# Two transformer layers on one core: units moved between the steps of a chain, dt's chain moved into the attention, the last expert's rows added by a one-hot product

## The chip, the cores and the metric

The kernel runs on 1 core of a Trainium2 chip. The metric is the device time of one execution in microseconds (us). A core has TensorE (matmul, PE in the profile; its loading of weights is PEld), VectorE (DVE), ScalarE (ACT), GpSimd (POOL) and SyncE (SP), which here only issues DMAs. All engines run their own instruction streams and wait for each other by semaphores. TensorE's clock is granted at one of two levels here, 1.2 or 2.4 GHz.

## The reference, cut to what matters

```python
# layer 1: adaLN, mLSTM + sparse attention, then a mixture of 32 experts, 4 of them for each of 256 tokens
logits = xf @ w_router + b_router;  vals, idx = top_k(logits, 4);  gate = softmax(vals)
y2[token] = sum over its 4 experts e of gate * (swiglu(h2 @ w_up[e] + b_up[e]) @ w_down[e] + b_down[e])
x = x + gt2 * rmsnorm(y2, g_post_ffn)
# layer 2: one input projection, then two branches side by side
h = rms_norm(x, norm_g) * (1 + scale) + shift;   proj = h @ w_in
q, k, v, z_att, q_idx, k_idx, w_idx, z_ssm, xbc, dt_raw, gate_logits = split(proj)
o_att = sparse_attention(rope(rms_norm(q)), rope(rms_norm(k)), v, index scores, top 64 keys) * silu(z_att)
y_att = o_att @ w_branch_att
xbc = silu(causal_depthwise_conv(xbc));  xs, bm, cm = split(xbc)
dt = softplus(dt_raw + dt_bias);  a = -exp(a_log)
y = (ssd(xs, dt, a, bm, cm) + d_skip * xs) * silu(z_ssm);  y = rms_norm over 4 groups(y)
y_ssm = y @ w_branch_ssm
merged = sigmoid(g_att) * y_att + sigmoid(g_ssm) * y_ssm
x = x + gate * (merged @ w_out)
```

256 tokens, D = 1024, all fp32; w_in of layer 2 is 1024 x 10084, ssd works in 2 chunks of 128 tokens, 32 heads, 4 groups.

## The kernel before, in words

The program is a row of blocks, one after another; in a block each engine has its own hand-written order, and a block ends when all engines have ended (the next block's first instructions follow some 0.5 us later).

**Experts** (L1340 to L1638). 32 experts, each with a fixed room of 96 rows. For each expert TensorE makes `up` (L1428), `turn` (L1439) and `down` (L1451) from weights that SP streams in; VectorE clips (`swiglu`, L1559 to L1566) and copies the result from PSUM to `ye` (`copy_y`, L1570); ScalarE stores `ye` to `y_dram` (`store`, L1517). GpSimd gathers each token's four rows from `y_dram` (L1398) in the order of `PLACES` (3, 2, 1, 0: place 3 is the token's lowest expert, place 0 its highest); VectorE multiplies them by the gates and adds (`add`, L1576, L1579), adds the bias product (`add_bias`, L1587), ScalarE squares (L1544), and so to the norm (L1486) and the next layer's norm.

**Units of layer 2.** All its weights go as units of 1024 x 256 (1 MB) through a ring of `RAWS` = 3 buffers (`load_unit`, L289, on SP). A unit in `SPLIT` is cut by ScalarE into a rounded part (`make_high`, L1655) and by VectorE into the rest (`make_low`, L1662), and TensorE makes three products of the rounded type from it; the buffer is free after `make_low`. A unit in `PLAIN` is multiplied as fp32, and its buffer is free only when TensorE has used it. Both are L1686 (by tokens) and L1698 (by columns), 48 instructions a split unit, 32 a plain one. `STAGES` = 3 pairs of high and low.

**Attention block** (L1822 on). Between the steps of the attention TensorE gives units (`give`), ScalarE takes them (`take`: silu to `azT` for four z units, L1861; four scaled copies, L1872, and later silu, L1849, for twelve xbc units), and GpSimd convolves (L1835). The order on TensorE before: give 2, turn index q and k, give 3, turn q and k (L1970), logits and scores 0, give 3, logits and scores 1, give 4, turn probabilities, give 2, turn, turn, give 2, attention product (L1995). VectorE multiplies `azT` by it at the end.

**State space block** (L2128 on). xbc is turned to token rows in nine sets (L2196, copies L2156), dt is made from 25 small VectorE operations (L2262 to L2279) to `adt`, `y = xs * dt` for all (L2286). Then eight pairs (chunk c, group g): `prepare` (L2213, L2216) makes the segment sums, VectorE the segment (L2306), ScalarE its exp (L2165), VectorE M (L2315), TensorE y (L2252); between them 16 fills, which are units for z and the two gates. After the pairs fills 16 to 19 (`w_branch_att`), gated into `mer` (L2353).

**Last block** (L2350 on). y is turned (L2384) and split into yh and yl (L2417, L2441), eight units of `w_branch_ssm` (L2394), merge (L2452 to L2455), four units of `w_out`, the addition to xT (L2461), turn (L2406) and output.

## Time and profile before

| what | us |
|---|---|
| median of 3 runs (lowest, highest) | 1860.7 (1860.04, 1865.69) |
| the profiled execution, whole | 1861.18 |
| its span | 1859.4 |
| TensorE busy | 1740.1 (94%) |
| VectorE, ScalarE, GpSimd busy | 555.9, 415.5, 106.4 |
| experts | about 289 to 1360 |
| layer 2 | about 1379 to 1859 |

Mean granted clock of TensorE 0.972 of 2.4 GHz. A row of the timeline gives start and length in us, engine, line, operation, written tile and read tiles, shapes and count, and in brackets the idle time before it with what ended it. A busy time of matmuls is modelled at its end, so the distance between starts says more than the length. A row of windows gives, for a stretch, its length and then each engine's busy time in it.

### The profile page before, as it was taken

The page shows a single profiled execution, that of the slowest core. Times are in us where ns is not written, and L with a number is a line of the kernel's source. Part 1 is how long each engine was busy: PE and PEld are TensorE (multiplying, and loading weights), DVE is VectorE, ACT ScalarE, POOL GpSimd, SP SyncE. Part 2 cuts the span into 40 slices and gives each one's busy share as a digit, 9 for nine tenths or more (in the row PEclk, how much of TensorE's full clock was granted, in tenths as well). Part 3 has the DMA queues.
Part 4 walks back from the last instruction along what each step waited for, and adds up shares of the span by engine and source line. Part 5 has one row for each costly group of instructions (what it writes and reads, how often), then busy time and mean ns, then how long its engine had stood idle before and what let it go on. Part 6 is the DMA issues. An engine that isn't in the chain of part 4 may idle for free. (4 is left out here: it accounts for less than half of the span.)

```text
span 1859.4 us, 39736 instructions
## 1 busy us (share of the span) xinstructions
PE 1740.1 (94%) x17331; PEld 1017.3 (55%) x17331; DVE 555.9 (30%) x770; ACT 415.5 (22%) x692; POOL 106.4 (6%) x121
## 2 busy tenths in 40 slices
PE   6999998999999999999999999999859798799888
PEld 4875652343434434343443434344449787698888
DVE  2273172121111112111111211111346551676754
ACT  2344152000000000000000000000034266355442
POOL 0111020000000000000000000000000044110000
PEclk9999989999999999999999999999979899899999
DMA  9987395999999999999999999999616243333452
GB/s 344 345 286 244 133 338 210 388 396 407 401 397 399 399 398 395 400 398 393 392 403 404 394 399 397 399 398 408 226 51 196 63 135 93 113 116 112 136 148 80
DMA packets 187878, 545.45 MB, mean 293 GB/s; under 512 B 16216, under 2 KB 90216, under 8 KB 154952
## 3 DMA queue, kind: packets, MB, share of 16 engines
q1 hardware_dynamic: 172432, 519.49, 74.0%
q10 hardware_dynamic: 10968, 15.40, 2.3%
q0 software_dynamic: 4416, 9.69, 1.6%
q8 instruction: 44, 0.72, 0.2%
q14 instruction: 18, 0.15, 0.0%
HBM read 526.06 MB, written 17.84 MB: 293 GB/s over the span
## 5 line engine op out<-in xcount | busy, mean ns | idle before, releaser
L1428 PE MATMUL ps<-ring_low,xg 128*32 128x512 f32 x3072 | 344.6, 597 | 0.0
L1428 PE MATMUL ps<-first_ring,xg 128*32 128x512 f32 x3072 | 335.4, 592 | 0.0
L1559 DVE TENSOR_SCALAR gl<-ps 128x768 f32<-128x768 f32 x32 | 30.6, 957 | 684.1 <-PE ps L1428 684.1
L1428 PEld LDWEIGHTS ps<-first_ring,xg 128*32 128x32 f32 x3072 | 99.5, 110 | 230.1 <-issue 230.1
L1428 PEld LDWEIGHTS ps<-ring_low,xg 128*32 128x32 f32 x3072 | 96.4, 110 | 206.6 <-issue 200.8
L1451 PE MATMUL ps<-first_ring,aT 128*32 128x256 f32 x3072 | 173.3, 382 | 2.3 <-ACT aT L1510 2.3
L1451 PE MATMUL ps<-raw_more,aT 128*32 128x256 f32 x3072 | 171.6, 379 | 0.0
L1451 PEld LDWEIGHTS ps<-first_ring,aT 128*32 128x32 f32 x3072 | 100.4, 111 | 82.5 <-issue 20.2
L1504 ACT ACTIVATE sg<-gl 128x768 f32<-128x768 f32 x32 | 27.0, 844 | 510.8 <-DVE gl L1559 510.8
L1451 PEld LDWEIGHTS ps<-raw_more,aT 128*32 128x32 f32 x3072 | 99.9, 110 | 65.9
L1662 DVE TENSOR_TENSOR low<-ring_low,high 128x2048 fp32r<-128x2048 f32 x42 | 98.7, 2350 | 121.5 <-ACT high L1655 121.0
L1509 ACT ACTIVATE aT<-ps 128x576 f32<-128x576 f32 x32 | 20.8, 650 | 445.5 <-PE ps L1439 435.7
L1655 ACT ACTIVATE high<-ring_low 128x2048 fp32r<-128x2048 f32 x42 | 80.4, 1915 | 65.8 <-PE ps L2394 20.5
L1570 DVE COPY ye<-ps 128x768 f32<-128x768 f32 x32 | 30.6, 957 | 212.1 <-PE ps L1451 212.1
L1698 PE MATMUL ps<-hT,ring_low 128*128 128x256 f32 x384 | 86.1, 386 | 0.0
L1698 PEld LDWEIGHTS ps<-hT,ring_low 128*128 128x128 f32 x384 | 74.5, 195 | 10.6 <-ACT xbc L1872 0.3
L1398 POOL DMA_INDIRECT got<-y_dram,dest x8 | 7.6, 952 | 1075.8 <-DMA y_dram<-ye 1074.6
L1698 PE MATMUL ps<-inh,high 128*128 128x256 f32 x320 | 49.0, 293 | 16.1 <-ACT azT L1861 7.8
L321 PE MATMUL ps<-hT,first_ring 128*128 128x256 f32 x256 | 58.7, 389 | 1.8 <-ACT hT L514 1.8
L321 PEld LDWEIGHTS ps<-hT,first_ring 128*128 128x128 f32 x256 | 49.2, 194 | 11.5 <-issue 4.7
L1698 PEld LDWEIGHTS ps<-inh,high 128*128 128x128 f32 x320 | 43.2, 198 | 17.1 <-ACT azT L1861 8.1
L1835 POOL TENSOR_TENSOR xbc<-xbc,taps 128x512 f32<-128x512 f32 x36 | 46.1, 1279 | 102.5 <-ACT xbc L1872 100.5
(487 smaller groups left out, 1879.6 us busy)
## 6 DMA issues: line engine op xcount, KB each, us to landing
first_ring<-in_w_up_dram SPq DMA_DIRECT2D x128, 1024.0 KB, 6.6
ring_low<-in_w_up_dram SPq DMA_DIRECT2D x128, 1024.0 KB, 6.3
raw_more<-in_w_down_dram SPq DMA_DIRECT2D x64, 1024.0 KB, 6.7
first_ring<-in_w_down_dram SPq DMA_DIRECT2D x64, 1024.0 KB, 6.7
ring_low<-in_w_in_dram SPq DMA_DIRECT2D x39, 1024.0 KB, 5.3
first_ring<-in_w_ada_dram SPq DMA_DIRECT2D x7, 2048.0 KB, 20.3
ring_low<-in_w_ada_dram SPq DMA_DIRECT2D x5, 2048.0 KB, 18.2
y_dram<-ye ACTq DMA_DIRECT2D x32, 288.0 KB, 5.7
```

The costliest lines, as they stand in the source:

```text
L321: mm = pe.matmul(ps[:, bank, (j % 2) * SEQ:(j % 2 + 1) * SEQ], slots[n % len(slots)][:, k, j * P:(j + 1) * P], src[:, k, :], start=(k == 0 ...
L1398: pool.indirect_dma_start(got[:, t, BUFFER[j], :], None, y_dram[0:TOTAL, :], bass.IndirectOffsetOnAxis(dest[:, t, j:j + 1], 0))\
L1428: mm = pe.matmul(ps[32 * q:32 * q + 32, u, :], xg[:, k, 32 * block_of:32 * block_of + 32], w[:, :, 256 * f:256 * f + 256], start=False, st ...
L1451: mm = pe.matmul(ps[32 * q:32 * q + 32, 5 + u, 0:256], aT[:, f, 32 * block_of:32 * block_of + 32], w[:, 256 * part:256 * part + 256], star ...
L1504: act.activation(sg[:], gl[:], ACT.Sigmoid, scale=ALPHA).then_inc(s(tag, "sig_ready"), 1)
L1509: act.activation(aT[:, 0:6, :], flat[:, :, 0:ROWS], ACT.Copy).then_inc(s(tag, "aT_ready"), 1)
L1559: dve.tensor_scalar(gl[:], ps[:, 0:3, 0:256], LIMIT, None, ALU.min).then_inc(s(tag, "glu_ready"), 1)
L1570: dve.tensor_copy(ye[:], ps[:, 5:8, 0:256]).then_inc(s(tag, "ye_copied"), 1)
L1655: act.activation(high[:, s_ % STAGES], raw2[u % RAWS], ACT.Copy).then_inc(sm("u_high"), 1)
L1662: dve.tensor_tensor(low[:, s_ % STAGES], raw2[u % RAWS], high[:, s_ % STAGES].bitcast(F32), ALU.subtract)\
L1698: mm = pe.matmul(ps[:, bank, j * SEQ:(j + 1) * SEQ], a[:, k, j * P:(j + 1) * P], x[:, k, :], start=(i == 0), stop=(i == len(todo) - 1))
L1835: ins = pool.tensor_tensor(c, c, taps[:, i % 2, tap], ALU.add)
```

## The change

- The order of units in layer 2: two z units, then the twelve xbc units, then the other two z units. Unit 7 (100 columns wide) and the first two units of `w_branch_att` (40, 41) are plain now. 39 units are split, where 42 were.
- The attention: give 2, turn index, give 2, turn q, give 1, logits and scores 0, give 3, logits and scores 1, give 4, turn, give 2, turn, give 1, turn, give 1, product. ScalarE takes both first z units before it squares the second half of q. dt's chain stands in this block, on VectorE before the scores and after the probabilities. Only three columns of the taps are cleared. Gating azT has moved to the next block.
- The state space block: cumulative products first, the nine sets in another order over three banks, copied by ScalarE (six) and VectorE (three), fill 0 before the first `prepare`, y multiplied pair by pair. Fills 16 and 17 read azT unsplit; 18 and 19 go to the last block, between the turns of y.
- Output: the first output unit does six row blocks of both column halves, then two.
- Experts: the last expert's rows are not stored. A one-hot of its rows times gate (`picks`, `picks3`) is made and turned ahead of the first expert, and the rows are added to the bias product in PSUM; place 0 is gathered behind place 1 with a gate that is zero for those tokens. VectorE adds place 1 before it copies the last expert's result. ScalarE fetches the Sqrt table during the last expert.

```diff
-UNITS2 += halves("w_in_2", 0, P_ZA) + halves("w_in_2", 0, P_ZA + 512)
+UNITS2 += halves("w_in_2", 0, P_ZA)
 U_XBC = len(UNITS2)
 UNITS2 += sum((halves("w_in_2", 0, P_XBC + 512 * n) for n in range(6)), [])
+UNITS2 += halves("w_in_2", 0, P_ZA + 512)
-PLAIN = {0, 1} | set(range(U_XBC, U_ZS))
+PLAIN = {0, 1, U_ZA - 1} | set(range(U_XBC, U_ZS - 2)) | {U_ATT, U_ATT + 1}
...
                 for j in PLACES:
-                    pool.wait_ge(s("", "ye_stored"), 32 * (NE - j))
+                    pool.wait_ge(s("", "ye_stored"), 32 * (NE - max(j, 1)))
...
+                def last_rows():
+                    for t in range(TT):
+                        at = slice(t * P, (t + 1) * P)
+                        pe.matmul(ps[:, 2 * t, :], picks[:, at], ye[0:ROWS, 0:2, :].rearrange("p u n -> p (u n)"),
+                                  start=False, stop=True, skip_group_check=True)
+                        pe.matmul(ps[:, 2 * t + 1, 0:256], picks[:, at], ye[0:ROWS, 2, :], start=False, stop=True,
+                                  skip_group_check=True)
+                        for u in range(3):
+                            mm = pe.matmul(ps[:, 2 * t + 1, 256:512], picks3[:, u, at], ye[ROWS:P, u, :], start=False,
+                                           stop=(u == 2), skip_group_check=True)
+                        mm.then_inc(s("", "bias_summed"), 1)
+                pe.wait_ge(sm("hot31_ready"), TT)
+                for t in range(TT):
+                    at = slice(256 + t * P, 256 + (t + 1) * P)
+                    pe.matmul(ps[0:ROWS, 5, at], li[:, t, 0:ROWS], idn, start=True, stop=True)
+                    for u in range(3):
+                        mm = pe.matmul(ps[ROWS:P, 5 + u, at], li[:, t, 32 * u:32 * u + 32], idn, start=True, stop=True)
+                mm.then_inc(sm("hot31_turned"), 1)
                 up("", 0)
...
                 turn("", NE - 1)
+                pe.wait_ge(sm("bdn_in"), 16)
+                down_bias(range(3), False)
                 down("", NE - 1)
-                pe.wait_ge(sm("bdn_in"), 16)
-                down_bias("")
+                down_bias(range(3, 4), False).then_inc(s("", "bias_started"), 1)
+                pe.wait_ge(s("", "bias_started"), 1)
+                pe.wait_ge(s("", "ye_copied"), NE + 1)
+                last_rows()
...
                 turned("", NE - 1)
-                store("", NE - 1, 0, NE - 1)
+                act.activation(sg[:, 0, 0:1], cst[:, C_ONES:C_ONES + 1], ACT.Sqrt).then_inc(s("", "sig_ready"), 1)
...
                 add("", 3)
                 add("", 2)
+                add("", 1)
                 dve.wait_ge(s("", "ye_stored"), (NE - 1) * 32)
                 copy_y("", NE - 1)
-                add("", 1)
+                add("", 0)
                 add_bias("")
-                add("", 0)
...
# attention block, ScalarE
-                    make_high(act, U_ZA + 2)
                     act.wait_ge(sm("var_ready"), 1)
                     S.done(act, act.activation(var[:], var[:], ACT.Sqrt), sm("dev_ready"))
-                    for t in range(TT):
-                        S.done(act, act.activation(sq2[:], qkv[:, t, 0:NH * HD], ACT.Square), sm("head_sq"))
-                        if t == 0:
-                            make_high(act, U_ZA + 3)
-                        act.wait_ge(sm("head_sums"), t + 1)
-                    S.done(act, act.activation(ssum[:], ssum[:], ACT.Sqrt), sm("head_rms"))
+                    S.done(act, act.activation(sq2[:], qkv[:, 0, 0:NH * HD], ACT.Square), sm("head_sq"))
                     take(2)
                     act.wait_ge(sm("i_turned"), 1)
...
-                    take(3)
+                    act.wait_ge(sm("head_sums"), 1)
+                    S.done(act, act.activation(sq2[:], qkv[:, 1, 0:NH * HD], ACT.Square), sm("head_sq"))
+                    act.wait_ge(sm("head_sums"), 2)
+                    S.done(act, act.activation(ssum[:], ssum[:], ACT.Sqrt), sm("head_rms"))
+                    take(2)
...
# state space block, TensorE and VectorE
+                    pe.wait_ge(sm("az_gated"), 1)
+                    fill(0)
+                    pe.wait_ge(sm("xs_ready"), 6)
+                    pe.wait_ge(sm("xs_copied"), 3)
                     prepare(0)
                     for i, (c, g) in enumerate(PAIRS):
-                        fill(2 * i)
+                        if i:
+                            fill(2 * i)
...
-                    for t in range(TT):
-                        yv = y[:, t, :].rearrange("p (h q) -> p h q", h=SH)
-                        ins = dve.tensor_tensor(yv, xs[:, t, :].rearrange("p (h q) -> p h q", h=SH),
-                                                dts[:, t, :].unsqueeze(2).to_broadcast([P, SH, SP]), ALU.mult)
                     for i, (c, g) in enumerate(PAIRS):
+                        V.link(dve, dve.tensor_tensor(heads(y[:, c, gw]), heads(xs[:, c, gw]),
+                                                      dts[:, c, gh].unsqueeze(2).to_broadcast([P, GH, SP]), ALU.mult))
...
# last block, TensorE
+                    turn(range(4))
+                    unit_by_columns(pe, U_ATT + 2, 4, None, (inh, inl))
+                    turn(range(4, 8))
+                    unit_by_columns(pe, U_ATT + 3, 5, None, (inh, inl))
```

## Rows read from the trace of the kernel before

**Rows 1.** Windows: us of PE, PEld, DVE, ACT, POOL; PEclk, DMA share, GB/s.
```profile
320.00:1300.00 980.00, 980.00 (x12094) 401.76 (x12086) 140.86 (x150) 77.29 (x150) 2.00 (x2) 1.00 1.00 398
...
1430.00:1584.10 154.10, 132.16 (x707) 118.74 (x707) 69.37 (x142) 81.42 (x178) 48.71 (x37) 0.93 0.31 96
1584.10:1620.40 36.30, 28.78 (x194) 26.20 (x195) 22.27 (x36) 14.95 (x20) 5.87 (x3) 0.83 0.45 138
1620.40:1723.30 102.90, 99.89 (x795) 94.09 (x794) 73.56 (x75) 51.21 (x42) 9.51 (x5) 1.00 0.37 114
1723.30:1780.50 57.20, 43.47 (x338) 41.59 (x337) 43.04 (x48) 28.47 (x31) 0.00 (x0) 0.94 0.46 133
```

**Rows 2.** Waits of PE, 1300 to 1860: who for whom; total, times, longest.
```profile
PE ps L1486 <- DVE gl L1627: 14.7, 1, 14.7
...
PE ps L1698 <- ACT azT L1861: 7.8, 1, 7.8
PE ps L2213 <- DVE y L2286: 6.7, 1, 6.7
PE ps L1953 <- ACT qT L1905: 4.6, 1, 4.6
PE ps L2196 <- PEq L1822: 4.4, 1, 4.4
...
PE ps L1938 <- ACT kT L1894: 3.5, 1, 3.5
PE ps L1698 <- issue: 3.4, 1, 3.4
```

**Rows 3.** Windows: unit 7, a split unit of the pair loop, a piece of half clock.
```profile
1424.54:1430.00 5.46, 5.46 (x50) 5.33 (x48) 2.29 (x1) 1.91 (x1) 0.00 (x0) 1.00 0.59 187
1612.00:1617.84 5.84, 5.84 (x52) 5.84 (x51) 4.52 (x2) 0.25 (x1) 2.07 (x1) 1.00 0.58 180
1433.00:1435.00 2.00, 2.00 (x11) 2.00 (x10) 1.86 (x5) 1.72 (x2) 1.10 (x1) 0.50 1.02 329
```

**Rows 4.** Timeline of the attention block: four plain units back to back.
```profile
1508.74 27.79 PE L1698 MATMUL ps<-hT,ring_low 128*128 128x256 f32 x128
```

**Rows 5.** Timeline at the start of the experts.
```profile
289.22 1.47 PE L1422 MATMUL ps<-bup,one 96*32 96x512 bf16 x12 [5.03 <-ACT xg L1500]
```

**Rows 6.** Timeline at the end of the experts, ScalarE.
```profile
1355.85 1.06 ACT L1544 ACTIVATE xsel<-hT 128x1024 f32<-128x1024 f32 x1 [0.82 <-DVE hT L1579]
...
1357.35 1.28 ACT L1547 ACT_TABLE_LOAD   x1 [0.36 <-DVE ssq L1623]
1358.65 0.20 ACT L1547 ACTIVATE ssq<-ssq 128x2 f32<-128x2 f32 x1
```

**Rows 7.** DMA issues, 1334.5 to 1336: median us from issue to landing.
```profile
got<-y_dram,dest POOLq DMA_INDIRECT x2, 7.7
```

**Rows 8.** Timeline of the attention block, VectorE: first and last of 18 on q.
```profile
1451.51 0.28 DVE L2034 RECIPROCAL ssum<-ssum 128x20 f32<-128x20 f32 x1 [0.41 <-ACT ssum L1885]
...
1462.26 0.32 DVE L1816 TENSOR_TENSOR qkv<-rt 128x160 f32<-128x160 f32 x1
```

**Rows 9.** Timeline, VectorE: a 128x1024 product alone and beside GpSimd.
```profile
1453.35 1.23 DVE L2038 TENSOR_TENSOR qkv<-qkv,bc 128x1024 f32<-128x1024 f32 x1
...
1524.11 2.23 DVE L2077 TENSOR_TENSOR sq<-sq,es 128x1024 f32<-128x1024 f32 x1
```

**Rows 10.** Timeline at the start of the state space block, VectorE.
```profile
1593.55 6.03 DVE L2286 TENSOR_TENSOR y<-xs,dts 128x2048 f32<-128x2048 f32 x2
```

**Rows 11.** Timeline of the pair loop: `prepare` of the fourth pair.
```profile
1644.07 0.49 PE L2213 MATMUL ps<-xbc 128*128 128x128 f32 x2 [0.46 <-DVE xbc L2306]
```

**Rows 12.** Timeline behind the pairs, VectorE: y scaled.
```profile
1749.77 4.62 DVE L2344 TENSOR_TENSOR y<-y,gs 128x2048 f32<-128x2048 f32 x2
```

**Rows 13.** Timeline at the end: the last two xT.
```profile
1853.14 1.00 DVE L2461 SCALAR_TENSOR_TENSOR xT<-ps,mod,xT 128x256 f32<-128x256 f32 x2 [4.75 <-PE ps L1698]
```

**Rows 14.** DMA issues, 1329 to 1331: median us from issue to landing.
```profile
ring_low<-in_w_in_dram SPq DMA_DIRECT2D x2, 1024.0 KB, 15.3
```

More of the change, by code:

```diff
@@ L1311, in _ @@
                     V.link(dve, dve.tensor_single_scalar(flag[:], fl, float(ROWS), ALU.is_gt))
+                    V.link(dve, dve.memset(first_row, 0))
                     for r in range(PER):
@@ L1829, in _ @@
                 def _(pool):
-                    G.done(pool, pool.memset(taps[:], 0.0), sm("taps_zero"))
-                    for i in range(HALVES - ZHALVES):
-                        pool.wait_ge(sm("half_taken"), ZHALVES + i + 1)
+                    G.done(pool, pool.memset(taps[:].rearrange("p a b c t -> p (a b c) t")[:, :, 0:3], 0.0), sm("taps_zero"))
+                    for i in range(XBC1 - XBC0):
+                        pool.wait_ge(sm("half_taken"), XBC0 + i + 1)
                         c = xbc[:, 2 * i:2 * i + 2, :]
@@ L1915, in _ @@
                     turned(2, P0[:, :, P:SEQ])
+                    take(1)
                     turned(3, P1)
-                    take(2)
-                    for i in range(HALVES - ZHALVES - 2, HALVES - ZHALVES):
-                        silu(i)
+                    take(1)
                 @block.tensor
@@ L2254, in _ @@
                         mm.then_inc(sm("y_made"), 1)
-                    for f in range(16, 20):
+                    for f in range(16, 18):
                         fill(f)
@@ L2321, in _ @@
                         make_low(dve, U_ZS + 2 * i + 3)
-                        if i == len(PAIRS) - 1:
-                            dve.wait_ge(sm("in_high"), 2)
-                            V.done(dve, dve.tensor_tensor(inl[:], azT[:], inh[:].bitcast(F32), ALU.subtract), sm("in_low"))
                         dve.wait_ge(sm("y_made"), i + 1)
@@ L2338, in _ @@
                     V.done(dve, dve.tensor_scalar(gs[:], gs[:], 1.0 / GW, EPS, ALU.mult, ALU.add), sm("gs_ready"))
-                    make_low(dve, U_ATT + 2)
+                    dve.wait_ge(sm("in_high"), 2)
+                    V.done(dve, dve.tensor_tensor(inl[:], azT[:], inh[:].bitcast(F32), ALU.subtract), sm("in_low"))
                     dve.wait_ge(sm("gs_rms"), 1)
```

274 lines of the change are left out of this document (155 added, 119 removed).

## The prediction, made before the changed kernel ran

> **What bounds the kernel now.** I read the windows by stage first, since one share of busy time over 1859 us says nothing about a stage of 50. In the expert loop TensorE works all 980 of 980 us at the full clock [rows 1]. The change touches that loop nowhere, and none of the waits listed for TensorE lies in it. The second layer is different: TensorE works 132.2 of 154.1 us around the attention, 28.8 of 36.3 at the start of the state space part, 99.9 of 102.9 in its pair loop and 43.5 of 57.2 from the last pair to the branch product [rows 1]. So TensorE sets the end everywhere, and what can be won is what it waits. The list of its waits gives the four places that the change is about: 14.7 us after the experts, 7.8 behind ScalarE's azT, 6.7 behind VectorE's y, 4.6 behind a copied probability tile [rows 2]. A wait costs more than its length. After the block change at 1430 the clock stood at half, 1.2 GHz, in 1433 to 1435 [rows 3]; half speed for some 3.4 us costs 1.7 us. I take 1.7 for every wait above 1.5 us that goes or comes.
>
> Unit prices. A unit that is not split takes 27.8/4 = 7.0 us of TensorE, a split one 5.8, with 1.9 of ScalarE and 2.3 of VectorE besides [rows 3, 4]. I walk through the change in order of time, always in the times of before; a sum at the end collects the differences.
>
> **Start of the experts.** TensorE now first turns the one-hot of the last expert: 8 fp32 products of 128 columns. Nothing in the trace is like it at half speed; from the prices of a unit (32 instructions of 256 columns in 7.0 us) one instruction of 128 columns takes 0.11, and 0.22 at half speed, so 16 take 3.5 us. It can begin at about 288.2, while the first product of the experts began at 289.22, released by ScalarE's xg [rows 5]. It is late by 2.5 us, less about 0.7 because the clock rises earlier: **+1.8** (bounds: 0 if it fits before xg, +2.5). The four small VectorE operations before it are hidden: they are under 1 us together, and behind the last of them ScalarE still had a bias copy and an xsel copy to make; if they were not, they would cost that 1 us.
>
> **End of the experts.** Before, the last expert's rows go to memory and are gathered back; the squares of the second half start at 1355.85, then a table load of 1.28, root, diagonal, and TensorE, 14.7 us after its last bias product, at 1359.8 [rows 2, 6]. After, the rows are added from SBUF by products, and the gather of place 0 no longer waits for a store. If the rows were all that counted: last copy at 1343.1, products 2 x 2.6 us (for each half of the tokens one of 512 columns and four of 256, at the 0.43 that 256 columns cost in a plain unit), 1348.3, addition 1.3, square 1.25, then 1.2 of root and diagonal without the table load, which is fetched earlier: TensorE at 1352.4, 7.4 us gained. But VectorE now adds place 1 **before** it copies the last expert's result, and the gather of place 1 landed late, 7.7 us after issue in the median of its two, of which the second was issued at 1334.8: at about 1342.7 [rows 7]; unit loads and the last weights fill the queues then. So: addition until 1344.0, copy until 1345.0, TensorE has idled since 1341.2 and works the products at half clock, 7.0 us, until 1352.1, addition 1353.3, square 1354.6, TensorE at 1356.2: **-3.6** (bounds -7.4 and -1.5, the latter if two more gathers behind it make the landing 2 us later).
>
> **First projections.** Unit 7 is no longer split: 5.46 us before [rows 3]; 32 instructions of 100 columns at 0.11 (48 took 5.46) make 3.7. The block ended with VectorE's copy right behind it, and SP's next load, now behind this unit instead of behind its low part, is issued in 0.4 us: **-1.7** (0 to -2.7, the latter if columns alone counted).
>
> **Attention.** The work of TensorE is the same: four split units, twelve plain, the small products. What moves are the waits.
> - The wait of 7.8 [rows 2] was for azT, and azT was behind the squares of q, which waited for VectorE's index chain and two splits. Now ScalarE takes azT straight after the first square, and two plain units, 14.1 us, lie under the norm and rotation of q. That chain ran from 1451.5 to 1462.6 [rows 8]. Its root now waits for a square that is behind azT and iqT, plus a table load: 1451.4, the same time. TensorE comes to the turning of q at 1459.6 and waits until 1462.6: 3.0 us.
> - GpSimd now convolves the first xbc unit, 4 us, at 1456 to 1460, beside this chain, where before it began at 1476. Beside such an operation VectorE's 128x1024 product took 2.23 instead of 1.23 [rows 9]. Two such delays: +2.0 (0 to 4.0). The Trainium skill says the same of the mechanism (GPSIMD Engine Reference, Specifications): GpSimd shares its SBUF interfaces with VectorE and contends with instructions that have two SBUF inputs; by it the chain would not be slowed where an operand is in PSUM, which none here is.
> - The wait of 3.5 before the index logits goes under the unit given between; the one of 4.6 goes under unit 22, since ScalarE turned the probabilities in 1.0 us and has the length of a unit for it.
> - Against that stands a rule of the Trainium skill (ScalarE: Activation LUTs, What ACT_TABLE_LOAD costs): a switch of tables costs a drain of about 1.38 us beside the load of 1.28. The change adds one switch for the second root and one for exp(A). The trace does not agree: the load of 1.28 began at 1357.35 and the root behind it at 1358.65, 0.02 after its end [rows 6]. By the page the root would come 1.4 later and the wait be 4.4 instead of 3.0.
>
> Sum: waits of 15.9 (7.8 + 3.5 + 4.6) become 5.0, three half-clock stretches become one: -10.9 - 3.4 = -14.3. The end: the gating of azT (2.3 us) and the last silu stood between the last product and the next block, 4.4 us of waiting [rows 2]; now the block closes 0.6 behind TensorE: -3.8. Further, the index chain loses 2 us of contention with a memset of 3072 columns, hidden. Unhidden remains a piece of half clock at the next start, which I don't count. With 0.9 kept back for ScalarE's heavier end: **-17.2** (bounds: -21 without contention or wait, -9 if ScalarE paces the last four units).
>
> **Start of the state space part.** It took 36.3 us from 1584.1 to 1620.4 [rows 1]. dt's 25 small operations ran in the shade of the transposes, but y for both halves, 6.0 us, stood in front of the first product [rows 10], and that then ran at half clock. After: cumulative products 0.9, nine sets of transposes with copies on two engines 5 (paced by VectorE, which gates azT first, 2.3), fill 0 5.8, preparation 2.4, state product 1.0, wait for the segment 0.7, preparation 2.3, fill 1 5.8, offset and y products 2.6: 26.5. **-9.9** (bounds -12 and -6; the last if all transposes run at half clock).
>
> **Pair loop.** y's product is now made pair by pair: 0.75 by the old row (6.03/8), 0.69 by xd's; 0.72. Is it hidden? The next preparation waited 0.46 us for VectorE's segment although a whole fill lay between [rows 11]: VectorE's chain from y to segment is the longer path by that much in each of pairs 1 to 6. So nothing hides it: 6 x 0.72 = **+4.3** (0 to +10).
>
> **Last pair to branch product.** Unit 40 is no longer split, so ScalarE and VectorE have no split in front of the last M, and TensorE no longer waits for that one. Units 40 and 41 read azT itself, so TensorE does not wait for inh and inl (3.4) [rows 2] and goes on, 2 x 7.0. VectorE then has inl 2.3, the scaling of y 4.6 [rows 12], two low parts 4.6 and two gatings: it ends at 1754.9, 4.1 us after TensorE, and sets the block's end. Behind it units 42 and 43 lie between the transposes, which took 11.4 us with their copies before unit 44; after it 17.5 with both units in them (half clock 1.9, twice 2.0, twice 5.8). Branch product at 1772.9 instead of 1780.5, and at full clock from its start (1.7): **-9.3** (bounds -12 and -5).
>
> **Tail.** The first output unit does six rows of both columns before the last two: -0.8. The last four xT instead of two wait for the last unit, two more operations of 0.5 [rows 13]: +1.0. **+0.2**.
>
> Sum: 1.8 - 3.6 - 1.7 - 17.2 - 9.9 + 4.3 - 9.3 + 0.2 = -35.4. The profiled execution took 1861.2 (span 1859.4, 1.8 around it), half a microsecond over the median 1860.7. So 1825.3, which I put at **1825.5**.
>
> **Rivals.**
> - *The forecast*, with its own range 1815 to 1835: 0.66.
> - *The new order of the attention moves the wait instead of filling it*: contention takes all of GpSimd's time, and ScalarE, with the same copies and more table loads, gives bank after bank late. For it speaks that ScalarE is the engine named in three of the four waits [rows 2]; against it that it works 81 of 154 us there [rows 1]. The stage gives 9 instead of 17.2: 1834. 0.14.
> - *VectorE becomes the bound of the pair loop*: it works 73.6 of 102.9 us [rows 1], so by sum it has room, but by chain it has none. If the added product also delays the split of the next unit, each of six pairs loses 2.5 us more: +15, 1840. 0.12.
> - *The one-hot product does not shorten the end of the experts* (gathers land later still, half clock): no gain there, 1829. 0.06.
> - *Slower: the ring of three raw buffers.* A plain unit holds its buffer until its product is done, so its successor's load has only two plain units, 14.1 us. The list of waits names no DMA [rows 2], so loads land in time now; where the queues were full two of them took 15.3 us [rows 14]. At a landing of t each of twelve units loses t - 14.1. The change would be slower by over 0.3% only from t = 14.1 + 41/12 = 17.5 us on; then +41 - 35, that is 1866. Before, the same twelve plain units showed no such wait. 0.02.
>
> The range takes 1810 (all lower bounds that don't exclude one another) to 1841: **1811 to 1841**. 0.3% is 5.6 us, which three runs within 5.7 us can about tell from no change. Faster by more: 0.95; within: 0.03; slower: 0.02.
>
> **What would show it.** TensorE begins with 16 small products before the first expert; its wait after the experts falls to about 4 + 4 around the last products; the first wait in the attention is about 5 us before the turning of q (128x128 of qkv), none behind azT; the first xd follows a 128x512 product of 0.7 us; the wait before the segment products in the loop is 1.1 to 1.2 instead of 0.4; VectorE's two last gatings end some 4 us behind unit 41. Wrong would be: a wait of the unit products for a DMA, pairs longer than 18 us on average, or gathers that land after 1345.

## The result, and the profile after

| what | us |
|---|---|
| before, median of 4 runs | 1863.1 (1860.0 to 1865.7) |
| after, median of 4 runs | 1836.9 (1834.5 to 1838.5) |
| ratio, 95% interval | 0.9854 (0.9842 to 0.9867) |
| the profiled execution of after, its span | 1836.7, 1834.9 |

The change takes 26.3 us off; forecast were 35.4 off (1825.5), with a range of 1811 to 1841. Between the two profiled executions lie 24.5 us (1861.2 to 1836.7).

Both totals hide losses. Windows of the trace of after for the attention block, the start of the state space block and the pair loop, as in [rows 1]; us of PE, PEld, DVE, ACT, POOL, then PEclk, DMA share, GB/s:

```profile
1435.18:1571.69 136.51, 126.90 (x707) 114.35 (x707) 82.93 (x166) 83.97 (x181) 48.98 (x36) 0.96 0.40 123
1571.69:1598.39 26.70, 24.59 (x194) 22.53 (x195) 15.88 (x15) 12.69 (x15) 5.70 (x3) 1.00 0.49 152
1598.39:1705.66 107.27, 100.02 (x794) 94.08 (x794) 77.90 (x82) 51.21 (x42) 9.53 (x5) 1.00 0.38 118
```

The first window begins with the block's first product. That of [rows 1] begins 1.6 us earlier, with a wait at the change of blocks that after has too (1.62); its block's first product in before:

```profile
1431.63 1.23 PE L1698 MATMUL ps<-inh,high 128*128 128x256 f32 x8 [1.63 <-PEq L1715]
```

So the attention block takes 136.5 instead of 152.5 us and the start of the state space block 26.7 instead of 36.3. The pair loop takes 107.3 instead of 102.9: TensorE works as long as before, and idles more. TensorE's waits in after, as in [rows 2] (who for whom; total, times, longest):

```profile
PE ps L1735 <- PEq L220: 9.7, 1, 9.7
PE ps L2027 <- DVE qkv L1870: 9.3, 1, 9.3
PE ps L2433 <- PEq L2202: 7.0, 1, 7.0
PE ps L1524 <- DVE gl L1676: 5.4, 1, 5.4
PE ps L2277 <- DVE xbc L2357: 5.3, 7, 1.1
PE ps L1494 <- DVE li L1635: 5.3, 1, 5.3
PE ps L1482 <- DVE ye L1612: 4.3, 1, 4.3
...
PE ps L2305 <- DVE xd L2348: 2.8, 3, 0.9
```

The four waits of before are gone. New are one of 9.3 in front of the turning of q, one of 7.0 at the start of the last block, 4.3 in front of the one-hot product, and ten small ones in the pair loop. The first row, 9.7 at the start of layer 2, is the same in both kernels.

**End of the experts.** Timeline of after:

```profile
1343.38 1.28 DVE L1622 SCALAR_TENSOR_TENSOR hT<-got,gate,hT 128x1024 f32<-128x1024 f32 x1 [9.38 <-DMA got<-y_dram,dest]
1346.38 1.28 DVE L1622 SCALAR_TENSOR_TENSOR hT<-got,gate,hT 128x1024 f32<-128x1024 f32 x1 [1.71 <-DMA got<-y_dram,dest]
1347.58 0.95 DVE L1612 COPY ye<-ps 128x768 f32<-128x768 f32 x1
...
1348.68 2.05 PE L1482 MATMUL ps<-ye,picks 96*128 96x512 f32 x2 [4.29 <-DVE ye L1612]
...
1357.22 2.92 PE L1487 MATMUL ps<-ye,low_high 32*128 32x256 f32 x6
...
1363.07 1.28 ACT L1589 ACT_TABLE_LOAD   x1 [0.36 <-DVE ssq L1672]
```

The copy of the last expert's result stands behind two additions that wait for gathers. TensorE has been idle for 4.3 us then and makes the products from 1348.7 to 1360.1, 11.4 us, at half clock (granted 0.50 over this stretch; two instructions of 512 columns in 2.05 us). And the Sqrt table, fetched at 1332.3, is loaded again in front of the root. Between them stands one more table load, behind the branch and in front of the squares:

```profile
1334.16 1.28 ACT L1586 ACT_TABLE_LOAD   x1 [0.33 <-issue]
```

**The q chain.** Timeline of after, VectorE and GpSimd:

```profile
1457.40 0.33 DVE L1866 TENSOR_TENSOR rt<-qkv,sin 128x160 f32<-128x160 f32 x1
1457.76 1.43 DVE L1867 TENSOR_TENSOR rt<-qkv,cos 128x160 f32<-128x160 f32 x1
1459.23 1.31 DVE L1868 TENSOR_TENSOR rt<-qkv,sin 128x160 f32<-128x160 f32 x1
1460.58 1.31 DVE L1869 TENSOR_TENSOR qkv<-rt 128x160 f32<-128x160 f32 x1
1461.92 0.33 DVE L1870 TENSOR_TENSOR qkv<-rt 128x160 f32<-128x160 f32 x1
```
```profile
1457.75 3.95 POOL L1889 TENSOR_TENSOR xbc<-xbc,taps 128x512 f32<-128x512 f32 x3 [22.63 <-ACT xbc L1929]
1464.66 4.23 POOL L1889 TENSOR_TENSOR xbc<-xbc,taps 128x512 f32<-128x512 f32 x3 [2.96 <-ACT xbc L1929]
```

Three additions of GpSimd, three VectorE operations of 1.3 to 1.4 us instead of 0.33; the second three meet three more. The chain takes 17.0 us from the reciprocal to the end, where it took 11.1 [rows 8].

**The last block's start.** Timeline of after:

```profile
1733.05 6.47 SPq L291 DMA_DIRECT2D ring_low<-in_w_branch_ssm_dram  x3
1735.48 1.40 DVE L2401 TENSOR_TENSOR ring_low<-ring_low,ps 128x512 f32<-128x512 f32 x2
...
1739.96 3.65 PE L2433 MATMUL ps<-cst,y 128*128 128x128 f32 x16 [6.95 <-PEq L2202]
```

TensorE is done at 1733.0, VectorE at 1736.9, and the block closes only behind SP, whose three issues last until 1739.5.

**Start of the experts.** Timeline of after:

```profile
286.12 1.91 ACT L1243 ACTIVATE bup<-b 32x2048 bf16<-32x2048 f32 x1 [1.26 <-DVE b L1303]
...
289.88 0.74 PE L1494 MATMUL ps<-cst,li 128*96 128x128 f32 x2 [5.25 <-DVE li L1635]
...
293.08 0.62 PE L1436 MATMUL ps<-bup,one 96*32 96x512 bf16 x3
```

ScalarE now waits 1.26 us for VectorE's last split of b_up, which the small operations on the last expert's rows precede; and the expert's own products start 3.9 us behind [rows 5], 1.3 of which lie ahead of every change (next paragraph).

**A caution for all stage times.** With the same code, layer 1 ended over 4 us apart between profiled executions (the first step of the norm before the router at 235.0 in before, 236.1 in after, 239.4 in the kernel of the first experiment, which has before's code up to there), with more half clock in 150 to 240 in the later ones (mean granted clock 0.96, 0.94 and 0.92). Stage times below are therefore counted from the scaled hT of that norm (VectorE, 128x256 x8, at 248.90 in before and 250.17 in after), so 1.3 us of the later starts in after belong to no change.

### The profile page after: what moved, and what is told of

Read it like the earlier page. It is cut to its first block and busy times, and to the rows that moved or that the text cites. A ratio compares the mean times of both kernels' runs of the same rounds, so it can differ in the third digit from the quotient of the medians.

```text
span 1834.9 us, 39709 instructions
## 1 busy us (share of the span) xinstructions
PE 1740.6 (95%) x17319; PEld 1014.9 (55%) x17319; DVE 565.7 (31%) x784; ACT 413.1 (23%) x691; POOL 106.6 (6%) x121
## 5 line engine op out<-in xcount | busy, mean ns | idle before, releaser
L1711 DVE TENSOR_TENSOR low<-ring_low,high 128x2048 fp32r<-128x2048 f32 x39 | 91.4, 2346 | 75.2 <-ACT high L1704 74.8
L1704 ACT ACTIVATE high<-ring_low 128x2048 fp32r<-128x2048 f32 x39 | 74.7, 1915 | 45.3 <-PE ps L2451 17.3
L348 POOL DMA_DIRECT2D mrows<-mrow x56 | 28.0, 508 | 187.1 <-ACT mrow L341 187.1
L1453 PEld LDWEIGHTS ps<-cst,gl 128*128 128x128 f32 x192 | 20.4, 140 | 26.4 <-issue 26.4
```

Source lines behind the costliest of these rows:

```text
L348: eng.dma_start(mrows[at:at + 4, :], mrow[32 * q:32 * q + 1, i % 2, :].rearrange("a (j p) -> a j p", p=P))\
L1704: act.activation(high[:, s_ % STAGES], raw2[u % RAWS], ACT.Copy).then_inc(sm("u_high"), 1)
L1711: dve.tensor_tensor(low[:, s_ % STAGES], raw2[u % RAWS], high[:, s_ % STAGES].bitcast(F32), ALU.subtract)\
```

## Experiments

In this table: the ratio to the runs of before made together with it, with its interval, and lengths in us, read from each profiled execution: from the scaled hT to the copy of expert 30's result (start), from there to TensorE's products for the norm (end), from there to the first turn of xbc in the state space block (attention), from there to the turning of y (state space), and the rest.

| kernel | ratio | start | end | attention | state space | rest |
|---|---|---|---|---|---|---|
| before | 1 | 1077.3 | 33.6 | 224.3 | 186.3 | 89.0 |
| after | 0.9854 | 1079.2 | 36.2 | 206.8 | 167.6 | 94.9 |
| 1 layer 2 only | 0.9823 (0.9809 to 0.9837) | 1076.0 | 33.7 | 206.4 | 167.1 | 95.2 |
| 2 experts only | 1.0008 (0.9995 to 1.0022) | 1078.9 | 33.9 | 225.8 | 186.2 | 89.3 |
| 3 copy before place 1 | 0.9820 (0.9805 to 0.9835) | 1079.6 | 29.0 | 207.4 | 168.0 | 94.8 |
| 4 convolution later | 0.9820 (0.9802 to 0.9838) | 1079.7 | 33.1 | 200.3 | 167.6 | 94.9 |
| 5 two loads later | 0.9825 (0.9804 to 0.9846) | 1079.1 | 36.1 | 206.8 | 165.3 | 94.2 |
| 6 y's product moved | 0.9829 (0.9816 to 0.9843) | 1079.6 | 36.9 | 206.4 | 163.2 | 95.5 |
| 7 start of the experts | 0.9836 (0.9822 to 0.9849) | 1076.1 | 36.2 | 207.0 | 167.6 | 95.0 |
| 8 additions in halves | 1835.5 us, one run | 1079.6 | 33.3 | 206.4 | 167.6 | 95.1 |
| 9 all five | 0.9709 (0.9696 to 0.9722) | 1076.2 | 26.6 | 200.0 | 160.5 | 95.0 |
| 10 and squares moved | 0.9691 (0.9677 to 0.9704) | 1076.2 | 27.8 | 201.3 | 154.9 | 94.9 |
| 11 and one low part moved | 0.9674 (0.9661 to 0.9688) | 1076.2 | 27.9 | 201.2 | 152.9 | 94.2 |

The intervals of 5, 6 and 7 overlap that of after, those of 3 and 4 do not; there the stage that was edited, and its row in the list of waits, carry the verdict, and the sum of all (9) bears it out. A stage that was not edited also differs from profile to profile, the end of the experts by up to 3.8 us (experiment 1 says how).

**1 and 2. The parts apart.** One kernel has every edit of layer 2 and none of the experts', the other the reverse.

> Only the changes of layer 2; the experts, their prelude and the store of the last expert are those of before. Theory (read from the trace of after): layer 2 gives about 31 us of its own, and the expert part takes 4.6 to 5.7 of them away; so this kernel is 30 to 32 us below before and 4 to 6 us below after. Rival (the expert part pays, as predicted, -1.8): this kernel is slower than after by 1 to 2 us, 24 to 25 below before. A difference between two profiled executions of which 1.1 us stood on TensorE at 231 already, ahead of every changed operation, says that part of the shift at the start may belong to no change: then the prelude here starts its first expert at the same time as in before, to 0.3 us, or is late by 1.1 here too.

> Only the changes of the experts and their prelude; layer 2 is that of before. Theory: 4 to 6 us slower than before: the first expert starts 2 to 3 us late (the 16 small products and VectorE's small operations in front of the last split of b_up), TensorE's products for the norm start 2.6 us later still against the last expert. Rival (prediction): 1 to 2 us faster than before. If the two parts add up, this difference and that of the kernel with layer 2 alone sum to the -26 of the whole change, within 1.5 us; if not, the ring of unit loads around the end of the experts couples them.

Layer 2 alone: 0.9823, some 33 us off; the experts' part alone: 1.0008, which is no difference that these runs can tell (0.9995 to 1.0022). So the part does not pay; the rival is out. My theory of 4 to 6 us slower missed too: it costs 1.6 us at the start and 0.3 at the end here. The two differences sum to -31.5, the whole gave -27, a gap over the 1.5 that I allowed, though each of the three is known only to some 2.5 us. The end of the experts explains 2.3 of it: the same code took 33.9 here and 36.2 in after. In seven profiles with this order on VectorE it took 33.1, 33.3, 33.9, 36.1, 36.2, 36.2 and 36.9. Where it took 36 or more, the second gather of place 1 let VectorE wait 1.6 us or more, and all of the one-hot product ran at half clock; in the others the wait was 0.4 us and TensorE began at full clock, and went to half for the second half of the tokens. In these others TensorE had also stood still for 1.0 to 1.5 us within its last `down`, which no engine of the profile explains; its last product before the wait came 2.4 us later, counted from expert 30's copy, so it idled 0.7 to 0.9 us in front of the one-hot product and not 4.2 to 5.0. Why the gathers and `down` differ between executions is open. The prelude's start differs, too: before's own profile shows 1077.3 where kernel 1, with the same code, shows 1076.0. Against the latter the new start costs 2.9 to 3.7 us.

**3. The order on VectorE.**

```diff
-                add("", 1)
                 dve.wait_ge(s("", "ye_stored"), (NE - 1) * 32)
                 copy_y("", NE - 1)
+                add("", 1)
                 add("", 0)
```

> After with one exchange on VectorE: copy of the last expert's result first, then the addition of place 1 (as the order was in before). Theory (the order on VectorE is what delays the one-hot product): the copy is at 1343.3 to 1344.3, TensorE's first product with picks at 1344.3 instead of 1348.7, with no half clock in front of it, so 5.7 us for both halves instead of 11.4; then VectorE has still place 1 and place 0 to add behind the gathers (landed 1343.4, 1346.4), until 1350.3, bias 1351.5, second bias 1352.8, and the products of the norm start at about 1358 instead of 1365.5: 6 to 8 us faster. Rival (the gathers' landing is what counts, and the product is hidden behind them): additions of place 0 end at 1350.3 in place of 1351.2, TensorE's clock stays half: 1 to 2 us faster at most.

The end takes 29.0 instead of 36.2 us, 7.2 less. Timeline of this kernel:

```profile
1348.87 2.47 DVE L1622 SCALAR_TENSOR_TENSOR hT<-got,gate,hT 128x1024 f32<-128x1024 f32 x2
1349.10 1.10 PE L1482 MATMUL ps<-ye,picks 96*128 96x512 f32 x2 [0.16 <-DVE ye L1612]
...
1353.53 1.56 PE L1487 MATMUL ps<-ye,low_high 32*128 32x256 f32 x6
```

TensorE waits 0.16 us instead of 4.3, keeps full clock (1.10 for what took 2.05), and both halves are done in 5.9 instead of 11.4 us. VectorE's additions now run beside them. The theory stands: what was late was the copy, not the gathers. Its size is less sure than the 7.2: this profile has the stand-still within `down`, and the kernels with the old order that have it too took 33.1 to 33.9 (4 and 8: 33.1 and 33.3), 4.1 to 4.9 more than 29.0. Without the stand-still, kernel 9 below takes 26.6 with this order, 1.3 of it gained by the table: some 8 us less than after.

**4. GpSimd off the q chain.**

```diff
+                    pool.wait_ge(sm("q_rotated"), TT)
                     for i in range(XBC1 - XBC0):
                         pool.wait_ge(sm("half_taken"), XBC0 + i + 1)
```

> After with GpSimd's first convolution held back until q and k are rotated (one more wait on GpSimd, none on another engine). Theory (GpSimd's additions beside VectorE stretch the chain): the six products of 128x160 on VectorE take 0.33 again instead of 1.27 to 1.43, the chain from the root to q's rotation 11 instead of 17 us, TensorE's wait in front of the turning of q falls from 9.3 to 3 to 4 us, and the kernel is 5 to 6 us faster. Rival 1 (the chain is slow for ScalarE's sake: squares, root and table load in its new place): the wait stays over 7 us and the time the same within 1 us. Rival 2 (the convolutions are then late and ScalarE's buffers wait for them): the wait falls, but a wait for a bank of the xbc units appears and the gain is under 2 us.

The rotation is as before, and the wait falls to 3.3; no other appears. First a row of VectorE, then one of the list of waits of this kernel:

```profile
1457.06 0.33 DVE L1867 TENSOR_TENSOR rt<-qkv,cos 128x160 f32<-128x160 f32 x1
```
```profile
PE ps L2028 <- DVE qkv L1870: 3.3, 1, 3.3
```

The attention takes 6.5 us less. Both rivals are out: ScalarE has the same order here, and the convolutions, all later, keep nobody waiting. The 3.3 that stay are the 3.0 that the prediction had without contention.

**8. What the contention is.** Each of GpSimd's additions is made in two halves.

```diff
-                            ins = pool.tensor_tensor(c, c, taps[:, i % 2, tap], ALU.add)
+                            half = [slice(0, 1), slice(1, 2)]
+                            G.link(pool, pool.tensor_tensor(c[:, half[0]], c[:, half[0]], taps[:, i % 2, tap, 0:1], ALU.add))
+                            ins = pool.tensor_tensor(c[:, half[1]], c[:, half[1]], taps[:, i % 2, tap, 1:2], ALU.add)
```

> After with each addition of the convolution on GpSimd made in two halves (six of 128x256 for a unit instead of three of 128x512); the same elements are added. In the trace of after six VectorE operations of the q chain are late by 0.94 to 1.10 us each, as many as GpSimd makes additions there, whatever their own length (0.33 or 0.43), and the 128x1024 product of before was late by 1.00 beside one addition too. Theory (a VectorE operation that starts while one of GpSimd's runs ends with it, so each addition costs VectorE at most one addition's length less its own): twelve operations are slow, each 0.6 to 0.7 us long instead of 1.3, 0.3 late each, 3.5 to 4.5 us in all, and TensorE's wait before q's turning falls from 9.3 to 7 to 8 us. Rival (VectorE gets a share of the bandwidth while GpSimd works): the same 6 us of lateness over the same 8 us of GpSimd, the wait as before, 9.1 to 9.3.

Timeline, VectorE and GpSimd:

```profile
1456.74 0.90 DVE L1867 TENSOR_TENSOR rt<-qkv,cos 128x160 f32<-128x160 f32 x1
1457.67 0.77 DVE L1868 TENSOR_TENSOR rt<-qkv,sin 128x160 f32<-128x160 f32 x1
1458.47 0.77 DVE L1869 TENSOR_TENSOR qkv<-rt 128x160 f32<-128x160 f32 x1
```
```profile
1456.73 0.72 POOL L1890 TENSOR_TENSOR xbc<-xbc,taps 128x256 f32<-128x256 f32 x1 [22.62 <-ACT xbc L1931]
1457.53 0.72 POOL L1891 TENSOR_TENSOR xbc<-xbc,taps 128x256 f32<-128x256 f32 x1
```

Twelve additions, twelve slow VectorE operations; the same product of 128x160 now takes 0.77 us, not 1.31: its time is that of one GpSimd addition, 0.72 here and 1.26 in after. A share of the bandwidth would have left it at 1.31. So the two engines take turns instruction by instruction, and the mechanism is shown. The size I expected of it was not: halves cost 0.80 us each in a row, not 0.66, a VectorE operation is late by 0.4 to 0.6, not 0.3, the total by 5.4 us, and the wait is 8.7, near the rival's. GpSimd waits in its turn: one addition of this kernel took 1.85 us beside a VectorE product that is 1.49 long when alone.

```profile
1460.07 1.94 DVE L2096 TENSOR_TENSOR qkv<-qkv,ssum 128x1280 f32<-128x1280 f32 x1
1460.74 1.85 POOL L1891 TENSOR_TENSOR xbc<-xbc,taps 128x256 f32<-128x256 f32 x1
```

The Trainium skill (SBUF — State Buffer, Who interferes with whom) calls the port pair that VectorE and GpSimd share an exclusive lock, and has a VectorE instruction with two SBUF inputs contend for it with a GpSimd instruction that reads SBUF. That one blocks the other for a whole instruction it says of VectorE's 2-port modes only. The trace shows it for these products with two inputs: one instruction each in turn.

**5. SP at the end of a block.**

```diff
-                    for u in range(U_ZS + 2, U_SSM + 3):
+                    for u in range(U_ZS + 2, U_SSM + 1):
                         load_unit(sp, u)
...
-                    for u in range(U_SSM + 3, len(UNITS2)):
+                    for u in range(U_SSM + 1, len(UNITS2)):
                         load_unit(sp, u)
```

> After with the loads of the second and third unit of w_branch_ssm issued in the last block instead of at the end of the state space block. Theory: SP's three issues there take 6.5 us (2.15 each, from 1733.05 on) and end at 1739.5, 2.6 us behind VectorE's last gating at 1736.9; TensorE's wait at the start of the last block falls from 7.0 to about 4.4 us and the kernel is 2 to 3 us faster. Rival 1 (the wait is VectorE's and the block change's own): the wait and the time stay. Rival 2 (the units now land too late for the branch product): the wait falls, and a wait for a load appears in front of the second or third unit of the branch product; no gain.

The list of waits of this kernel:

```profile
PE ps L2433 <- PEq L2202: 4.6, 1, 4.6
```

4.6 instead of 7.0, the state space part 2.3 us shorter, and no wait for a load behind it. The theory stands, in its size too. The ratio would allow more than these 2.3 us, but its interval (0.9804 to 0.9846) overlaps that of after.

**6. y's product in VectorE's own wait.** The product y = xs * dt of the first pair stands ahead of the loop, and that of each next pair behind the segment:

```diff
+                        if i + 1 < len(PAIRS):
+                            times_dt(i + 1)
                         make_low(dve, U_ZS + 2 * i + 2)
```

> After with one move on VectorE: the product y = xs * dt of the next pair stands right behind the segment of this one, where VectorE then waits 4.5 us for ScalarE's split, instead of between the last addition of a pair and the next xd. Theory (the +4.3 is the position, not the work): the seven waits before the segment sums fall from 5.3 to about 2 us in all, those behind xd from 2.8 to 0.7, and the kernel is 4 to 5 us faster. Rival (VectorE is the bound of the loop by its sum, and the product only moves the delay to the splits): the waits before the segment sums fall, but others before the unit products or y's product appear, and the time stays within 1 us.

The list of waits of this kernel, in which L2364 is the segment and L2355 xd:

```profile
PE ps L2277 <- DVE xbc L2364: 3.1, 7, 0.8
...
PE ps L2305 <- DVE xd L2355: 0.6, 3, 0.2
```

The waits fall from 5.3 to 3.1 and from 2.8 to 0.6, together by 4.4, the stage by 4.4: the same work, placed where VectorE waited 4.5 us for ScalarE's split, costs nothing. I had expected the first to fall to 2; VectorE's chain is still the longer path there. The number of waits stayed at ten; only their lengths fell.

**7. Start of the experts.** The last expert's small operations go behind `rest(2, NE)`, the one-hot is made in `got` instead of `li`, and TensorE turns it behind `up("", 0)`:

```diff
+                up("", 0)
                 pe.wait_ge(sm("hot31_ready"), TT)
...
                 mm.then_inc(sm("hot31_turned"), 1)
-                up("", 0)
```

> After with the start of the experts changed alone: VectorE's three small operations on the last expert's rows stand behind the last split of b_up, and TensorE turns the one-hot behind the first expert's up, where it waits for VectorE's clip in any case. Theory (from the first norm before the router, since the stretch ahead of it differs by up to 4 us between executions): the first product with the experts' weights comes 3 to 3.5 us earlier, 1 to 1.5 us come back at the second expert for the 16 products, 1.5 to 2.5 us faster in all. Rival (TensorE's first expert is bound by its first weights or by xg in any case): 0.5 us or less.

The start takes 1076.1 instead of 1079.2 us (1079.1 to 1079.7 in the kernels with the old start): 3.1 less, more than expected, since of the 2.9 us that TensorE waits for the second expert's xg (7.9 for two waits in before, 5.0 the first) all but 0.5 now hold the 16 products. It is as short as in kernel 1, which has no one-hot at all.

**9, 10 and 11. Together.** Kernel 9 has 3 to 7, and the Sqrt table fetched behind the branch that is not taken:

```diff
-                act.activation(sg[:, 0, 0:1], cst[:, C_ONES:C_ONES + 1], ACT.Sqrt).then_inc(s("", "sig_ready"), 1)
                 with flagged(act):
...
+                act.activation(ssq[:, 0:1], cst[:, C_ONES:C_ONES + 1], ACT.Sqrt).then_inc(s("", "sig_ready"), 1)
+                act.wait_ge(s("", "sig_ready"), NE + 1)
```

> After with all five changes: copy of the last expert's result before place 1 is added; the Sqrt table fetched behind the branch that is not taken, so that no second load stands before the root; start of the experts; first convolution behind the rotation of q; y's product behind the segment; loads of two units of w_branch_ssm in the last block. If the causes are independent the gains add: 6 + 1.3 + 2 + 6 + 4.5 + 2.5, that is about 20 to 23 us below after, 1814 to 1818. If they hide one another (all sit on TensorE's own line, so I expect not), less than 15. The table: theory (the second load comes from the branch between) says that no table load stands between the squares and the root; rival (the load comes with every use after a Square) says that it does.

> The kernel with the five changes, and the squares and their sum of each pair moved behind the segment of the next pair too. Theory: VectorE's chain from y's product on TensorE to the next segment is 1.4 us shorter; the seven waits before the segment sums fall from 3.1 to under 0.5 us, that behind xd from 0.6 to 0; 2.5 to 3.5 us faster than with the five changes, if nothing else is late: 1807. Rival (now VectorE's splits come late instead, since 2.1 us of products fill its wait for ScalarE's split of 4.5): the gain is under 1 us.

> As the kernel before it, and the low part of unit 43 moved from the end of the state space block to the last block. Theory: VectorE ends that block with the gating of unit 41, which waits for TensorE; the block closes 1.1 us earlier and TensorE's wait of 4.5 falls to about 3.3; since the low part then lies between the fourth and fifth yl, where VectorE waits for ScalarE, it costs nothing: 1 us faster again, 1806. Rival (the yl that it is put in front of pace the transposes): the wait of the second set of transposes grows by up to 2 us, no gain or a loss of 1.

Kernel 9 runs at 1810.2 us, 0.9709 of before: some 27 us below after, a little more than the 23 expected, so no gain hides another. Its timeline, ScalarE, between the squares and the root:

```profile
1354.18 0.19 ACT L1586 ACTIVATION_READ_ACCUMULATOR xsel<-hT 128x1 f32 x1
...
1354.76 0.20 ACT L1589 ACTIVATE ssq<-ssq 128x2 f32<-128x2 f32 x1 [0.39 <-DVE ssq L1672]
```

No table load is left there, so the squares alone bring none. Nor does the branch alone: in before, which has it and no fetch ahead of it, no table load stands in front of the squares. The fetch ahead of the branch brought two more, one in front of the squares and one in front of the root. That the load in front of the squares put another table in Sqrt's place would explain the last one; which table a load takes, the trace does not show. The end of the experts is 26.6, 7.0 below before. In kernel 10 the squares of a pair go into the same wait of VectorE; the state space part falls by 5.6 us, though the waits listed in the loop were only 3.7, and one of 0.9 is left. Windows over five pairs in the middle of the loop, first of kernel 9, then of kernel 10:

```profile
1588.18:1674.20 86.02, 83.34 (x661) 78.43 (x661) 65.44 (x69) 42.68 (x35) 9.52 (x5) 1.00 0.39 123
```
```profile
1587.60:1668.41 80.81, 80.81 (x663) 78.40 (x661) 67.39 (x68) 42.70 (x36) 9.52 (x5) 1.00 0.42 131
```

TensorE's idle 2.7 us are gone, and its busy time for the same work falls by another 2.5. The 2.7 were eight waits of 0.2 to 0.5, so a wait in a row of products cost here some 0.3 us beside its listed length. It goes by the wait and not by its length: in experiment 6 the waits became shorter but not fewer, and the stage gave just the 4.4 us that the list gave. The whole gives less than the stage: 1810.2 to 1807.2 us, or 0.9709 to 0.9691 (intervals that overlap), 3.0 to 3.4 us of the 2.5 to 3.5 expected. In the profile of kernel 10 the end of the experts and the attention, which have the same code, are 1.2 and 1.3 us longer.

Kernel 11 closes the state space block earlier, its wait falls from 4.5 to 2.6, and it runs at 1803.8 us, 0.9674: 3.3% below before and the fastest here. What is left in the list of waits of kernel 11:

```profile
PE ps L1735 <- PEq L220: 9.7, 1, 9.7
...
PE ps L1524 <- DVE gl L1676: 4.1, 1, 4.1
PE ps L2028 <- DVE qkv L1870: 3.3, 1, 3.3
PE ps L2449 <- PEq L2203: 2.6, 1, 2.6
```

## Why the prediction was right, and where it was not

The direction, the range and the place of most of the gain were right. Stage by stage, from the two profiles (the difference of the starts of the same work):

| term | forecast | measured |
|---|---|---|
| ahead of any change | 0 | +1.3 |
| start of the experts | +1.8 | +1.9 (3.2 to 3.7 against kernel 1) |
| end of the experts | -3.6 | +2.6 |
| layer 2 to the first projections' end | -1.7 | -2.2 |
| attention | -17.2 | -16.0 |
| start of the state space part | -9.9 | -9.6 |
| pair loop | +4.3 | +4.4 |
| last pair to branch product | -7.6 | -5.6 |
| tail, with the branch product's clock | -1.5 | -1.3 |
| sum | -35.4 | -24.5 |

The forecast put 1.7 us for the branch product's full clock into its -9.3 for the last pair. That gain lies behind the branch product's start, so here it stands in the last row (-7.6 - 1.7, and +0.2 - 1.7). It came: the first sixteen of these products took 3.3 us to the next group in before and take 1.9 in after. The first row is before, the second after:

```profile
1780.54 3.54 PE L2394 MATMUL ps<-yh,high 128*128 128x256 f32 x16 [3.54 <-issue]
```
```profile
1757.35 2.04 PE L2451 MATMUL ps<-yh,high 128*128 128x256 f32 x16
```

- **End of the experts: the step that failed, with the wrong sign and outside its bounds.** Seen from expert 30's copy, the copy of the last result was done 0.4 us later than forecast, so the landing of the gathers and VectorE's order were right. Then "works the products at half clock, 7.0 us": they took 11.4. I had laid 1.8 for half clock on 5.2 of products, about the flat price of every wait, but the products are 5.9 at full clock (experiment 3), and the clock stayed at half through all of them, which nearly doubles them. That is 4.4 us. The table load that was to be saved was not, 1.3 us. The rival for it (no gain there, 0.06) named later landings and half clock; in this profile it was the second, with the table load. Where the first half ran at full clock the end still took 33.1 to 33.9, no gain on before's 33.6 worth the name.
- **Start of the experts: the sum nearly right, its parts not.** "The four small VectorE operations before it are hidden" was wrong: against kernel 1, xg came 0.9 us later from the scaled hT, and ScalarE waited 1.26 us for VectorE. The products cost 2.2 (the first product with weights 4.3 us behind xg instead of 2.1), near the forecast.
- **Attention: the sum right within its bounds, the wait mis-sized.** TensorE waited for q, as forecast, and none stood behind azT. But 9.3 us instead of 5.0. "Two such delays: +2.0" counted the VectorE operations of the size in [rows 9]. What counts is GpSimd's instructions: six additions, six operations late by 0.94 to 1.10, 5.9 us. The upper bound of 4.0 was too low. The row of the Trainium skill that the prediction cited (GPSIMD Engine Reference, Specifications) names a 2-port mode of VectorE beside two SBUF inputs; the prediction left that out. In after, 128x64 operations with one SBUF input and constants took 1.26 and 1.29 instead of 0.20 beside GpSimd as well; whether they ran in such a mode the trace does not show. The rest of the block gave 3 us more than forecast: no other wait came, and ScalarE's heavier end, for which 0.9 were kept back, cost nothing.
- **Last pair to branch product: VectorE's end right, the block's not.** VectorE ended 3.9 us behind TensorE, forecast 4.1, and counted from the end of the pair loop 31.2 instead of 31.6. The step "and sets the block's end" left out SP: three issues of 2.15 us, the last of which ended 2.6 us behind VectorE. These 2.6 less the 0.4 by which VectorE was early are the missing 2.0, to 0.2 us; the transposes and the two units behind them took 17.4 for 17.5. Experiment 5 gives 2.4 us back.
- **Pair loop: the sum right and for the reason given, the place half right.** Nothing hid y's product in that place; experiment 6 shows that it was the place. All six delays of 0.7 us were to stand in front of the segment sums. Three do (waits of 0.9 to 1.1 us), the other three are in front of xd (0.9 instead of 0.2).
- **Start of the state space part: right** (26.7 us; the forecast's own terms add up to 26.5, and 36.3 less that is 9.8, not 9.9).
- **The rivals.** VectorE as the bound of the loop with the splits late: no sign of it, VectorE still waited 4.5 us for ScalarE in a pair. The ring of raw buffers: no wait for a load is in the list. The wait that only moves in the attention: half true, 9.3 of 15.9 us, with the price paid by other terms.
- The time came out where two smaller cases met, the one-hot product that does not pay and more contention; each had been put apart from the forecast with a small chance, none of them together. That it still lies within 1811 to 1841 is in part luck: two terms went beyond their bounds, the end of the experts (by 4.1 us) and the contention (by 1.9), and 3 us that the rest of the attention gave beyond its forecast paid for most of the 4.3 by which the wait for q was too short.

## What to carry to other kernels

Beside an engine that shares a port with the one on the critical path, count the other's instructions, not your own: each costs up to its whole length, so hold it back until the short chain is through. A stretch of half clock nearly doubles all the work in it (11.4 us for 5.9), so price it with that work; and order a copy that TensorE waits for ahead of additions that wait for DMAs. Where blocks end together, look for the engine that only issues: its last DMA issues can be the block's end.

## What was not expected of the hardware

- VectorE and GpSimd alternate by instruction: products of 0.33 us took 1.31 beside additions of 1.26 and 0.77 beside additions of 0.72.
- An issue of a load of w_branch_ssm costs SP 2.15 us in after, one of w_branch_att 0.37 in kernel 9; both are 1 MB, the former in rows of 128 elements, the latter of 256.
- Each wait of 0.2 to 0.5 us in a row of products cost TensorE some 0.3 us beside its listed length (eight waits of 2.7 us in all, 5.2 us of time in five pairs).
- A Sqrt table that had been fetched ahead of a branch that was not taken was loaded again (1.28 us) in front of the root, with one more table load in front of the squares; fetched behind the branch, it was loaded once.
- The same code up to the router's norm ended over 4 us apart between executions, with half clock in other places.
